# One selection matmul fills the inputs of two experts, where a transpose filled one

## Chip, cores and metric

The kernel runs on one core of a Trainium2 chip. The metric is the device time of one execution in microseconds (us).

## The reference

One layer of a decoder trunk on 320 tokens (256 of a prompt, 64 of samples), width 2048, all fp32. A token mixer comes first; the change does not touch it. Then a mixture of experts in two levels: each token goes to one of 4 groups, and there to 2 of 4 SwiGLU experts.

```python
g_val, g_idx = lax.top_k(g_prob, 1)
e_val, e_idx = lax.top_k(e_prob, TOP_K_EXPERT)
gates = g_val * e_val
combine = jnp.sum(jax.nn.one_hot(ids, N_EXPERTS, dtype=jnp.float32) * gates[..., None], axis=1)
hg = jnp.einsum('nd,edf->nef', xt, w_gate)      # 16 experts, D = 2048, F = 512
hu = jnp.einsum('nd,edf->nef', xt, w_up)
a = jax.nn.silu(hg) * hu * combine[:, :, None].astype(x.dtype)
out = jnp.einsum('nef,efd->nd', a, w_down)
x = layer_norm(ALPHA * x + out, ln2_g, ln2_b)
```

Every expert has 12 MB of weights (gate 4 MB, up 4 MB, down 4 MB), 192 MB in all, and each is read once.

## The kernel before

The mixer and its projections take roughly the first 395 us, the router the next 25, and the rest is the loop over the 16 experts, with which the change deals.

**Weights.** A ring of `SLOTS = 9` slots of 2 MB holds the experts' weights. The list `ORDER` gives the units in which they come: of expert e four units of gate and up (two transfers of 1 MB each), then the two down units of expert e-1 (one transfer of 2 MB each). SP issues the transfers in that order, in `load_half` (L380) and in `sp_experts` (L1060). From the tenth unit on it waits on `ring_used` for the matmuls that last read the slot. Before the tenth unit it waits for the gather of the first group's rows (L1049) and issues four loads of 1 MB for the layer norms (L1050 to L1053).

**Inputs of an expert.** The rows of one group of experts, up to 128 tokens, are gathered into `xg`. DVE's `pick(g)` writes `order` (L1486): for each of the group's four experts a matrix of zeros and ones that says which row stands at which of the expert's 64 places (`C = 64`); it is made 128 columns wide. It then makes `gated` from it. PE's `fill(e, j)` (L1189) makes four tiles of 128 features by 128 places for expert e, with a transpose that takes `order` in place of the identity; j runs over `FILLS = 4`, so that an expert needs 16 of them. ScalarE's `evict_fill(e, j)` (L1327) applies scale and bias of the layer norm and writes the first 64 columns of each to `xT[e % 2]`, one instruction per tile.

**PE's order.** All four fills of expert 0 stand ahead of the loop. In the loop over e, `gate_up(e, j)` (L1239, eight matmuls of 64 by 512, which read one unit) and `fill(e + 1, j)` take turns. Then come `turn_a(e - 1)` (L1249, transposes of the activations), `combine(e - 2)` (L1215), for the second expert of a group `weights_back(g)` (L1198), and `down(e - 1)` (L1263, 16 matmuls, which read the two down units). Behind the loop the same for the last expert, and `last_rows` (L1226).

**PSUM.** The fills of expert 0 use banks 0 to 3; all others use bank 7 (`MS`), so that `fill(e, j)` waits on `xT_ready` for the eviction of the fill before it.

**ScalarE's order.** For expert e: the evictions of fills 0 to 2 of expert e + 1, the Silu of expert e (L1361), the eviction of fill 3, the copy `aT` (L1334), for which `down` waits, and the copy `y_sb` (L1345).

Of the kernel before, what the change touches and what calls it, by code (L numbers as in the profile page):

```python
# [10 lines left out]
P = 128  # L11
# [26 lines left out]
def hybrid_trunk_kernel(nc, x_prompt, x_sample, state_conv, state_pool, w_in, conv_w, sgu_ln_g,  # L38
# [149 lines left out]
    G0 = YT_HI0  # L188
    xT = [at(f"xT{s}", G0 + s * 4 * KB, [P, PAIRS, 4, C]) for s in range(2)]
    y_sb = at("y_sb", G0 + 8 * KB, [P, HD])  # L190
    group_slot = at("group_slot", G0 + 12 * KB, [P, 3, P])
    order = at("order", G0 + 13 * KB + 512, [P, EG, P])
    gated = at("gated", G0 + 15 * KB + 512, [P, EG, 2, C])
# [977 lines left out]
    def pe_experts(pe):  # L1171
# [6 lines left out]

        def fill(e, j):

            g, k = where(e)
            pe.wait_ge(xn_ready, 2 * g + j // 2 + 1)
            pe.wait_ge(order_ready, g + 1)
            if e:
                pe.wait_ge(xT_ready, FILLS * e + j)
                pe.wait_ge(gatedT_ready, (e + 1) // EG)
            for c in range(4):
                col = HD * (j // 2) + 4 * (j % 2) + c
                last = pe.transpose(ps[:, fill_bank(e, j), P * c:P * (c + 1)],  # L1189
                                    xg[g % 2][:, col:HD * (j // 2 + 1):HK], order[:, k, :])  # L1190
            last.then_inc(xT_full, 1)

        def weights_back(g):

            pe.wait_ge(gated_ready, g + 1)
            pe.wait_ge(xT_ready, FILLS * (EG * g + 3))
            for k in range(EG):
                last = pe.transpose(ps[:, MS, P * k:P * (k + 1)],  # L1198
                                    gated[:, k, :, :].rearrange("p h s -> p (h s)"), ident[:, :])
            last.then_inc(gatedT_full, 1)  # L1200
# [28 lines left out]
        def gate_up(e, j):  # L1229
            i = AT[e, j]  # L1230
            pe.wait_ge(xT_ready, FILLS * e + j + 1)
            if e and j == 0:
                pe.wait_ge(a_ready, e)
            pe.wait_ge(unit_full[i % SLOTS], all_in(i))
            w = gu_w[i % SLOTS][:, :, :].rearrange("p g (c f) -> p g c f", c=4)
            for c in range(4):
                x = xT[e % 2][:, j, c, :]
# [34 lines left out]
        info(0, FACTS, info_made)  # L1272
        for j in range(FILLS):
            fill(0, j)
        for e in range(NE):
            g, k = where(e)
            for j in range(PAIRS):
                gate_up(e, j)
                if e + 1 < NE:
                    fill(e + 1, j)  # L1280
                if k == 0 and j == 1 and g < NG - 1:
# [39 lines left out]
    def act_experts(act):  # L1321
        def evict_fill(e, j):
            n = FILLS * e + j + 1
            act.wait_ge(xT_full, n)
            for c in range(4):
                hc = 4 * (j % 2) + c
                last = act.activation(xT[e % 2][:, j, c, :], ps[:, fill_bank(e, j), P * c:P * c + C],  # L1327
                                      ACT.Identity, bias=gbT[:, 1, j // 2, hc:hc + 1],
# [24 lines left out]
        for e in range(NE):  # L1353
            g, k = where(e)
            if e + 1 < NE:
                for j in range(FILLS - 1):
                    evict_fill(e + 1, j)
# [4 lines left out]
            if e + 1 < NE:  # L1362
                evict_fill(e + 1, FILLS - 1)
            if e:
# [103 lines left out]
    def dve_experts(dve, steps, link, rows):  # L1468
# [11 lines left out]
        def pick(g):  # L1480

            dve.wait_ge(told_ready, g + 1)
            if g:
                dve.wait_ge(xT_full, FILLS * EG * g)
                dve.wait_ge(gatedT_full, g)
            dve.scalar_tensor_tensor(out=order[:, :, :], in0=slots[:, :].unsqueeze(1).to_broadcast([P, EG, P]),  # L1486
                                     scalar=row_no[:, 0:1],
                                     in1=told[:, g, 1:1 + EG].unsqueeze(2).to_broadcast([P, EG, P]),
                                     op0=ALU.subtract, op1=ALU.is_equal).then_inc(order_ready, 1)
            dve.wait_ge(order_ready, g + 1)  # L1490
            for h in range(2):
                last = dve.tensor_tensor(gated[:, :, h, :], order[:, :, 0:C],
                                         told[:, g, 1 + EG:1 + 2 * EG].unsqueeze(2).to_broadcast([P, EG, C]),
                                         ALU.mult)
# [11 lines left out]
        def residual_rows(g):  # L1506

            x = xg[g % 2]
            if g == 0:
                dve.wait_ge(aln_in, 32)  # L1510
                steps.inc(dve.tensor_scalar(aln_g[:, :], aln_g[:, :], ALPHA, None, ALU.mult))
                link(dve.tensor_scalar(aln_b[:, :], aln_b[:, :], ALPHA, None, ALU.mult))
            dve.wait_ge(xT_full, FILLS * EG * (g + 1))
            link(dve.tensor_tensor(x[:, :], x[:, :], aln_g[:, :], ALU.mult))
# [264 lines left out]
```

## Time and profile before

| what | value |
|---|---|
| median of three runs | 905.77 us (904.85 to 905.96) |
| the profiled execution | 904.5 us, its span 902.5 us |
| PE busy | 830.9 us, 92% of the span |
| DVE, ScalarE, GpSimd busy | 283.7, 255.2, 22.7 us |
| read from HBM | 267.23 MB |

The span runs from the first to the last instruction of the profile; 2.0 us of the time lie outside it. PE's busy time counts a matmul from start to end, and a PE that waits for weights between two matmuls is idle. An fp32 matmul stands in the trace as two records, a transpose as one.

### The profile page before, as it was taken

The page shows a single profiled execution, that of the slowest core. Times are in us where ns is not written, and L with a number is a line of the kernel's source. Part 1 is how long each engine was busy: PE and PEld are TensorE (multiplying, and loading weights), DVE is VectorE, ACT ScalarE, POOL GpSimd, SP SyncE. Part 2 cuts the span into 40 slices and gives each one's busy share as a digit, 9 for nine tenths or more (in the row PEclk, how much of TensorE's full clock was granted, in tenths as well). Part 3 has the DMA queues.
Part 4 walks back from the last instruction along what each step waited for, and adds up shares of the span by engine and source line. Part 5 has one row for each costly group of instructions (what it writes and reads, how often), then busy time and mean ns, then how long its engine had stood idle before and what let it go on. Part 6 is the DMA issues. An engine that isn't in the chain of part 4 may idle for free.

```text
span 902.5 us, 11139 instructions
## 1 busy us (share of the span) xinstructions
PE 830.9 (92%) x4709; PEld 556.6 (62%) x4709; DVE 283.7 (31%) x389; ACT 255.2 (28%) x452; POOL 22.7 (3%) x37
## 2 busy tenths in 40 slices
PE   6999999999999999985999999999999888897884
PEld 6989999999999999974333333333333233333231
DVE  5273375335664343535002100412004030031203
ACT  5243332333223232332322222322223121222101
POOL 0000000000001000001000000000000000000000
PEclk9999999999999999996999999999999999999998
DMA  9643653654454884378999999999999999999960
GB/s 298 182 140 120 200 181 121 206 186 139 145 163 150 294 285 139 119 265 356 421 424 427 420 423 424 425 420 423 424 426 419 423 424 424 420 425 424 423 295 31
DMA packets 81595, 271.96 MB, mean 301 GB/s; under 512 B 5577, under 2 KB 58271, under 8 KB 59592
## 3 DMA queue, kind: packets, MB, share of 16 engines
q1 hardware_dynamic: 78618, 263.12, 75.0%
q0 software_dynamic: 1856, 5.28, 1.5%
q10 hardware_dynamic: 1078, 2.94, 1.0%
q8 instruction: 33, 0.54, 0.2%
q14 instruction: 10, 0.08, 0.0%
HBM read 267.23 MB, written 11.54 MB: 309 GB/s over the span
## 4 chain that ended last, share of the span: by engine, by line
PE 66%; DMA 20%; SPq 5%; DVE 4%; ACT 3%; issue 1%; POOLq 0%; POOL 0%; ACTq 0%; DVEq 0%
PE ps L1239 15%; DMA gu_w<-in_expert_w_up 14%; PE ps L458 12%; PE ps L460 11%; PE ps L459 11%; PE ps L1263 8%; SPq L380 4%; DMA down_w<-in_expert_w_down 4%; PE ps L1189 3%; DMA raw<-in_w_in 1%; ACT xT L1327 1%; DMA raw<-in_w_out 1%; PE ps L1126 1%; PE ps L485 1%; PE ps L486 1%
## 5 line engine op out<-in xcount | busy, mean ns | idle before, releaser
L1239 PE MATMUL ps<-gu_w,xT 128*64 128x512 f32 x1024 | 235.3, 601 | 26.8 <-DMA gu_w<-in_expert_w_up 26.2
L639 DVE TENSOR_TENSOR w_lo<-raw,w_hi 128x2048 fp32r<-128x2048 f32 x50 | 114.6, 2291 | 172.3 <-ACT w_hi L631 170.7
L1239 PEld LDWEIGHTS ps<-gu_w,xT 128*64 128x64 f32 x1024 | 74.9, 137 | 151.4 <-issue 146.6
L458 PE MATMUL ps<-xT_hi,w_hi 128*128 128x320 f32 x512 | 159.2, 311 | 0.0
L459 PE MATMUL ps<-xT_lo,w_hi 128*128 128x320 f32 x512 | 158.2, 309 | 0.0
L460 PE MATMUL ps<-xT_hi,w_lo 128*128 128x320 f32 x512 | 158.2, 309 | 0.0
L631 ACT ACTIVATE w_hi<-raw 128x2048 fp32r<-128x2048 f32 x49 | 93.8, 1914 | 209.4 <-DMA raw<-in_w_in 128.3
L1327 ACT ACTIVATE xT<-ps,gbT 128x64 f32<-128x64 f32 x256 | 82.4, 408 | 162.4 <-PE ps L1189 162.4
L1263 PE MATMUL ps<-down_w,aT 128*64 128x512 f32 x512 | 115.3, 602 | 4.6 <-ACT aT L1334 4.0
L1569 DVE TENSOR_TENSOR a_sb<-ps,a_sb 128x256 f32<-128x256 f32 x16 | 6.8, 425 | 298.5 <-ACT a_sb L1361 298.5
L458 PEld LDWEIGHTS ps<-xT_hi,w_hi 128*128 128x128 f32 x512 | 96.1, 188 | 0.5
L459 PEld LDWEIGHTS ps<-xT_lo,w_hi 128*128 128x128 f32 x512 | 96.1, 188 | 0.0
L460 PEld LDWEIGHTS ps<-xT_hi,w_lo 128*128 128x128 f32 x512 | 96.1, 188 | 0.0
L1263 PEld LDWEIGHTS ps<-down_w,aT 128*64 128x64 f32 x512 | 35.6, 138 | 80.6 <-issue 65.9
L458 PE MATMUL ps<-yT_hi,w_hi 128*128 128x320 f32 x256 | 79.8, 312 | 0.6 <-DVE yT_lo L799 0.6
L460 PE MATMUL ps<-yT_hi,w_lo 128*128 128x320 f32 x256 | 79.1, 309 | 0.0
L459 PE MATMUL ps<-yT_lo,w_hi 128*128 128x320 f32 x256 | 79.1, 309 | 0.0
L1189 PEld LDWEIGHTS ps<-order,xg 128*128 128x128 f32 x256 | 34.6, 197 | 52.4 <-issue 47.9
L1189 PE MATMUL ps<-order,xg 128*128 128x128 f32 x256 | 46.4, 308 | 3.6 <-DVE xg L1503 3.0
L458 PEld LDWEIGHTS ps<-yT_hi,w_hi 128*128 128x128 f32 x256 | 48.1, 188 | 0.9 <-DVE yT_lo L799 0.9
L459 PEld LDWEIGHTS ps<-yT_lo,w_hi 128*128 128x128 f32 x256 | 48.1, 188 | 0.0
L460 PEld LDWEIGHTS ps<-yT_hi,w_lo 128*128 128x128 f32 x256 | 48.1, 188 | 0.0
(241 smaller groups left out, 479.7 us busy)
## 6 DMA issues: line engine op xcount, KB each, us to landing
gu_w<-in_expert_w_gate SPq DMA_DIRECT2D x64, 1024.0 KB, 27.5
gu_w<-in_expert_w_up SPq DMA_DIRECT2D x64, 1024.0 KB, 30.9
down_w<-in_expert_w_down SPq DMA_DIRECT2D x32, 2048.0 KB, 31.2
raw<-in_w_in SPq DMA_DIRECT2D x34, 1024.0 KB, 5.3
raw<-in_w_out SPq DMA_DIRECT2D x16, 1024.0 KB, 5.4
tok<-in_x_prompt SPq DMA_DIRECT2D x2, 1024.0 KB, 6.2
z_rows<-tok ACTq DMA_DIRECT2D x2, 768.0 KB, 4.1
aln_g<-in_ln_g SPq DMA_DIRECT2D x1, 1024.0 KB, 4.2
```

The source lines that it names most:

```text
L380: sp.dma_start(gu_w[s][:, n, :].rearrange("p (c f) -> p c f", c=4), src[:, e, h, c:c + 4, :])\
L458: pe.matmul(out, wh[:, t, col], hi[:, kt, :], start=(n == 0 and t == 0), stop=False)
L459: pe.matmul(out, wh[:, t, col], lo[:, kt, :], start=False, stop=False)
L460: last = pe.matmul(out, wl[:, t, col], hi[:, kt, :], start=False, stop=(n == 1 and t == CK - 1))
L485: pe.matmul(out, wh[:, t, col], hi[:, kt, :], start=(n == 0 and t == 0), stop=False)
L486: pe.matmul(out, wh[:, t, col], lo[:, kt, :], start=False, stop=False)
L631: act.activation(w_hi[k][:, :], raw[k][:, :], ACT.Copy).then_inc(hi_ready, 1)
L639: dve.tensor_tensor(w_lo[k][:, :], raw[k][:, :], w_hi[k][:, :].bitcast(FP32), ALU.subtract)\
L1189: last = pe.transpose(ps[:, fill_bank(e, j), P * c:P * (c + 1)], xg[g % 2][:, col:HD * (j // 2 + 1):HK], order[:, k, :])
L1239: last = pe.matmul(ps[C * side:C * (side + 1), GU, :], x, w[:, :, c, FH * side:FH * (side + 1)], start=(j == 0 and c == 0), stop=(j == PAI ...
L1263: last = pe.matmul(ps[C * side:C * (side + 1), Y + q, :], aT[:, f % 2, f // 2, :], down_w[i % SLOTS][:, n, col:col + 512], start=(f == 0), ...
L1327: last = act.activation(xT[e % 2][:, j, c, :], ps[:, fill_bank(e, j), P * c:P * c + C], ACT.Identity, bias=gbT[:, 1, j // 2, hc:hc + 1], s ...
```

## The change

- `fill(pair, j)` takes the place of `fill(e, j)`. It multiplies the rows of `xg` with the selection of two neighbouring experts at once: 64 + 64 = 128 columns. It is an ordinary fp32 matmul and no transpose.
- `order` has 64 columns per expert (it had 128), so that two experts' columns lie side by side. It is written at 256 elements per partition in place of 512.
- `xT` is one tile with a place for both experts. ScalarE writes both from one tile of PSUM, 128 elements per instruction in place of 64, half as many instructions.
- Fills stand in the loop at odd experts only: behind `gate_up(e, j)` for odd e comes `fill((e + 1) // 2, j)`, for experts e + 1 and e + 2.
- Of the first pair only `fill(0, 0)` stands ahead of the loop; `fill(0, j + 1)` stands ahead of `gate_up(0, j)`.
- The counts in the waits follow. `weights_back(g)` waits for the same eviction as before, the fills that stand just ahead of it.

```diff
-    order = at("order", G0 + 13 * KB + 512, [P, EG, P])
+    order = at("order", G0 + 13 * KB + 512, [P, EG, C])
...
+        def fill(pair, j):
+
+            g, k = where(2 * pair)
             pe.wait_ge(xn_ready, 2 * g + j // 2 + 1)
             pe.wait_ge(order_ready, g + 1)
-            if e:
-                pe.wait_ge(xT_ready, FILLS * e + j)
-                pe.wait_ge(gatedT_ready, (e + 1) // EG)
+            if pair:
+                pe.wait_ge(xT_ready, FILLS * pair + j)
+                pe.wait_ge(gatedT_ready, pair // 2)
             for c in range(4):
                 col = HD * (j // 2) + 4 * (j % 2) + c
-                last = pe.transpose(ps[:, fill_bank(e, j), P * c:P * (c + 1)],
-                                    xg[g % 2][:, col:HD * (j // 2 + 1):HK], order[:, k, :])
+                last = pe.matmul(ps[:, fill_bank(pair, j), P * c:P * (c + 1)],
+                                 xg[g % 2][:, col:HD * (j // 2 + 1):HK],
+                                 order[:, k:k + 2, :].rearrange("p k s -> p (k s)"), start=True, stop=True)
             last.then_inc(xT_full, 1)
...
-        for j in range(FILLS):
-            fill(0, j)
+        fill(0, 0)
         for e in range(NE):
             g, k = where(e)
             for j in range(PAIRS):
+                if e == 0 and j + 1 < FILLS:
+                    fill(0, j + 1)
                 gate_up(e, j)
-                if e + 1 < NE:
-                    fill(e + 1, j)
+                if e % 2 and e + 1 < NE:
+                    fill((e + 1) // 2, j)
...
-                last = act.activation(xT[e % 2][:, j, c, :], ps[:, fill_bank(e, j), P * c:P * c + C],
+                last = act.activation(xT[:, :, j, c, :],
+                                      ps[:, fill_bank(pair, j), P * c:P * (c + 1)].rearrange("p (k s) -> p k s", k=2),
                                       ACT.Identity, bias=gbT[:, 1, j // 2, hc:hc + 1],
                                       scale=gbT[:, 0, j // 2, hc:hc + 1])
...
-            dve.wait_ge(xT_full, FILLS * EG * (g + 1))
+            dve.wait_ge(xT_full, FILLS * 2 * (g + 1))
```

The place at which the loop over the experts starts, on PE, before the change (`gu_w_52` to `gu_w_59` are slots of the ring; a row x4 is one fill, a row of `gu_w` x8 one `gate_up`):

```order
L1189 MATMUL ps<-order,xg_72 128x128 x16
L1239 MATMUL ps<-gu_w_52,xT_139 64x512 x8
L1189 MATMUL ps<-order,xg_72 128x128 x4
L1239 MATMUL ps<-gu_w_53,xT_139 64x512 x8
L1189 MATMUL ps<-order,xg_72 128x128 x4
L1175 MATMUL ps<-facts,group_slot 128x11 x3
L1239 MATMUL ps<-gu_w_54,xT_139 64x512 x8
L1189 MATMUL ps<-order,xg_72 128x128 x4
L1239 MATMUL ps<-gu_w_55,xT_139 64x512 x8
L1189 MATMUL ps<-order,xg_72 128x128 x4
L1239 MATMUL ps<-gu_w_56,xT_140 64x512 x8
```

The same place after it:

```order
L1189 MATMUL ps<-order,xg_72 128x128 x8
L1240 MATMUL ps<-gu_w_52,xT 64x512 x8
L1189 MATMUL ps<-order,xg_72 128x128 x4
L1240 MATMUL ps<-gu_w_53,xT 64x512 x8
L1175 MATMUL ps<-facts,group_slot 128x11 x3
L1189 MATMUL ps<-order,xg_72 128x128 x4
L1240 MATMUL ps<-gu_w_54,xT 64x512 x8
L1240 MATMUL ps<-gu_w_55,xT 64x512 x8
L1240 MATMUL ps<-gu_w_56,xT 64x512 x8
```

Two fills stand ahead of the first `gate_up` where there were four; the other two of the first pair stand behind the first and the second `gate_up`, and none stands behind the third and the fourth.

On ScalarE, from the fills of the first experts to the copy of `aT` of expert 0, before (`xT_139` and `xT_140` are the two buffers):

```order
L1327 ACTIVATE xT_139<-ps,gbT 128x64 x16
L1327 ACTIVATE xT_140<-ps,gbT 128x64 x12
L1361 ACT_TABLE_LOAD
L1361 ACTIVATE a_sb<-ps 128x256
L1327 ACTIVATE xT_140<-ps,gbT 128x64 x4
L1327 ACTIVATE xT_139<-ps,gbT 128x64 x12
L1361 ACTIVATE a_sb<-ps 128x256
L1327 ACTIVATE xT_139<-ps,gbT 128x64 x4
L1334 COPY aT<-ps 128x256
```

and after:

```order
L1329 ACTIVATE xT<-ps,gbT 128x2x64 x16
L1364 ACT_TABLE_LOAD
L1364 ACTIVATE a_sb<-ps 128x256
L1329 ACTIVATE xT<-ps,gbT 128x2x64 x12
L1364 ACTIVATE a_sb<-ps 128x256
L1329 ACTIVATE xT<-ps,gbT 128x2x64 x4
L1337 COPY aT<-ps 128x256
```

The evictions of expert 0's turn are gone, and those of expert 1's turn stand where they stood, four of them still between the Silu and the copy of `aT`, each twice as wide.

## Rows read from the trace of the kernel before

**Rows 1.** The page: GB/s in 40 equal slices of the span.

```profile
GB/s 298 182 140 120 200 181 121 206 186 139 145 163 150 294 285 139 119 265 356 421 424 427 420 423 424 425 420 423 424 426 419 423 424 424 420 425 424 423 295 31
```

**Rows 2.** Stretches: width, busy us of each engine, PEclk, DMA share, GB/s.

```profile
416.00:421.50 5.50, 1.56 (x6) 1.43 (x6) 3.61 (x14) 0.00 (x0) 0.00 (x0) 0.50 0.42 173
421.50:426.00 4.50, 3.96 (x18) 3.56 (x20) 1.21 (x2) 2.80 (x10) 0.00 (x0) 0.51 0.90 379
426.00:440.00 14.00, 14.00 (x72) 5.62 (x70) 0.46 (x4) 5.45 (x18) 1.03 (x1) 1.00 1.00 414
440.00:640.00 200.00, 195.56 (x922) 72.99 (x918) 32.12 (x43) 55.88 (x151) 3.06 (x3) 0.99 1.01 424
640.00:866.00 226.00, 196.81 (x903) 75.94 (x903) 36.09 (x47) 53.04 (x139) 5.01 (x5) 0.99 1.01 423
```

**Rows 3.** The chain that ended last: start us, us, what.

```profile
498.26 3.43 PE ps L1239 x16
...
524.33 3.43 PE ps L1239 x16
...
837.43 31.80 DMA down_w<-in_expert_w_down
...
869.27 3.68 PE ps L1263 x16
...
880.15 7.02 PE ps L1263 x32
```

**Rows 4.** Groups by shape on PE: count, busy us, mean ns, idle before.

```profile
L1239 PE MATMUL ps<-gu_w,xT 128*64 128x512 f32 x1024 | 235.3, 601 | 26.8 <-DMA gu_w<-in_expert_w_up 26.2 <-DVE a_sb L1569 0.5
...
L1189 PE MATMUL ps<-order,xg 128*128 128x128 f32 x256 | 46.4, 308 | 3.6 <-DVE xg L1503 3.0 <-issue 0.5
...
L574 PE MATMUL ps<-wsT,vtok 128*128 128x128 f32 x24 | 3.6, 273 | 0.0
```

**Rows 5.** The start of the experts in order of time: start, us, engine.

```profile
419.25 0.75 DVE L1486 SCALAR_TENSOR_TENSOR order<-slots,row_no,told 128x512 f32<-128x512 f32 x1
420.03 0.76 DVE L1492 TENSOR_TENSOR gated<-order,told 128x256 f32<-128x256 f32 x2
...
420.89 0.33 SPq L1050 DMA_DIRECT2D aln_g<-in_ln_g  x1
...
422.04 3.68 PE L1189 MATMUL ps<-order,xg 128*128 128x128 f32 x16 [3.04 <-DVE xg L1503]
...
429.32 0.71 PE L1189 MATMUL ps<-order,xg 128*128 128x128 f32 x4
...
429.96 3.65 PE L1239 MATMUL ps<-gu_w,xT 128*64 128x512 f32 x16
```

**Rows 6.** Groups by shape on ScalarE.

```profile
L1327 ACT ACTIVATE xT<-ps,gbT 128x64 f32<-128x64 f32 x256 | 82.4, 408 | 162.4 <-PE ps L1189 162.4
...
L709 ACT ACTIVATE pext<-ps 128x64 f32<-128x64 f32 x4 | 0.8, 266 | 0.0
...
L705 ACT ACTIVATE pnew<-ps 128x128 f32<-128x128 f32 x2 | 0.6, 296 | 0.0
```

**Rows 7.** In order of time, 460 to 470 us: SP's issues.

```profile
460.63 0.43 SPq L380 DMA_DIRECT2D gu_w<-in_expert_w_up  x1
...
468.81 0.33 SPq L380 DMA_DIRECT2D gu_w<-in_expert_w_gate  x1
```

**Rows 8.** DMA issues from 460 to 461 us: KB each, us to landing.

```profile
gu_w<-in_expert_w_up SPq DMA_DIRECT2D x1, 1024.0 KB, 14.8
```

**Rows 9.** PE in order of time, 701 to 711 us.

```profile
705.42 5.35 PE L1239 MATMUL ps<-gu_w,xT 128*64 128x512 f32 x16 [3.11 <-DMA gu_w<-in_expert_w_up]
```

**Rows 10.** Stretches around it and at expert 15, columns as in Rows 2.

```profile
844.00:864.00 20.00, 16.09 (x72) 5.67 (x70) 0.00 (x0) 1.25 (x2) 0.00 (x0) 1.00 1.02 428
...
705.00:709.00 4.00, 3.58 (x10) 1.44 (x12) 0.00 (x0) 0.00 (x0) 0.00 (x0) 0.59 1.03 438
```

**Rows 11.** PE in order of time, expert 15, where no fills stand.

```profile
859.58 3.65 PE L1239 MATMUL ps<-gu_w,xT 128*64 128x512 f32 x16 [1.31 <-DMA gu_w<-in_expert_w_up]
```

More of the change, by code:

```diff
@@ L188, in hybrid_trunk_kernel @@
     G0 = YT_HI0
-    xT = [at(f"xT{s}", G0 + s * 4 * KB, [P, PAIRS, 4, C]) for s in range(2)]
+    xT = at("xT", G0, [P, 2, PAIRS, 4, C])
     y_sb = at("y_sb", G0 + 8 * KB, [P, HD])
     group_slot = at("group_slot", G0 + 12 * KB, [P, 3, P])
-    order = at("order", G0 + 13 * KB + 512, [P, EG, P])
+    order = at("order", G0 + 13 * KB + 512, [P, EG, C])
     gated = at("gated", G0 + 15 * KB + 512, [P, EG, 2, C])
@@ L1177, in info @@
             last.then_inc(done, 1)
-        def fill(e, j):
-            g, k = where(e)
+        def fill(pair, j):
+            g, k = where(2 * pair)
             pe.wait_ge(xn_ready, 2 * g + j // 2 + 1)
             pe.wait_ge(order_ready, g + 1)
-            if e:
-                pe.wait_ge(xT_ready, FILLS * e + j)
-                pe.wait_ge(gatedT_ready, (e + 1) // EG)
+            if pair:
+                pe.wait_ge(xT_ready, FILLS * pair + j)
+                pe.wait_ge(gatedT_ready, pair // 2)
             for c in range(4):
                 col = HD * (j // 2) + 4 * (j % 2) + c
-                last = pe.transpose(ps[:, fill_bank(e, j), P * c:P * (c + 1)],
-                                    xg[g % 2][:, col:HD * (j // 2 + 1):HK], order[:, k, :])
+                last = pe.matmul(ps[:, fill_bank(pair, j), P * c:P * (c + 1)],
+                                 xg[g % 2][:, col:HD * (j // 2 + 1):HK],
+                                 order[:, k:k + 2, :].rearrange("p k s -> p (k s)"), start=True, stop=True)
             last.then_inc(xT_full, 1)
@@ L1195, in weights_back @@
             pe.wait_ge(gated_ready, g + 1)
-            pe.wait_ge(xT_ready, FILLS * (EG * g + 3))
+            pe.wait_ge(xT_ready, FILLS * (2 * g + 2))
             for k in range(EG):
@@ L1230, in gate_up @@
             i = AT[e, j]
-            pe.wait_ge(xT_ready, FILLS * e + j + 1)
+            pe.wait_ge(xT_ready, FILLS * (e // 2) + j + 1)
             if e and j == 0:
@@ L1236, in gate_up @@
             for c in range(4):
-                x = xT[e % 2][:, j, c, :]
+                x = xT[:, e % 2, j, c, :]
                 for side in range(2):
@@ L1321, in act_experts, with evict_fill @@
     def act_experts(act):
-        def evict_fill(e, j):
-            n = FILLS * e + j + 1
+        def evict_fill(pair, j):
+            n = FILLS * pair + j + 1
             act.wait_ge(xT_full, n)
@@ L1354, in act_experts @@
             g, k = where(e)
-            if e + 1 < NE:
+            if e % 2 and e + 1 < NE:
                 for j in range(FILLS - 1):
-                    evict_fill(e + 1, j)
+                    evict_fill((e + 1) // 2, j)
             act.wait_ge(ring_used, AT[e, PAIRS - 1] + 1)
@@ L1361, in act_experts @@
             act.activation(a_sb[:, :], ps[:, GU, 0:FH], ACT.Silu).then_inc(silu_ready, 1)
-            if e + 1 < NE:
-                evict_fill(e + 1, FILLS - 1)
+            if e % 2 and e + 1 < NE:
+                evict_fill((e + 1) // 2, FILLS - 1)
             if e:
@@ L1483, in pick @@
             if g:
-                dve.wait_ge(xT_full, FILLS * EG * g)
+                dve.wait_ge(xT_full, FILLS * 2 * g)
                 dve.wait_ge(gatedT_full, g)
-            dve.scalar_tensor_tensor(out=order[:, :, :], in0=slots[:, :].unsqueeze(1).to_broadcast([P, EG, P]),
+            dve.scalar_tensor_tensor(out=order[:, :, :], in0=slots[:, 0:C].unsqueeze(1).to_broadcast([P, EG, C]),
                                      scalar=row_no[:, 0:1],
-                                     in1=told[:, g, 1:1 + EG].unsqueeze(2).to_broadcast([P, EG, P]),
+                                     in1=told[:, g, 1:1 + EG].unsqueeze(2).to_broadcast([P, EG, C]),
                                      op0=ALU.subtract, op1=ALU.is_equal).then_inc(order_ready, 1)
@@ L1491, in pick @@
             for h in range(2):
-                last = dve.tensor_tensor(gated[:, :, h, :], order[:, :, 0:C],
+                last = dve.tensor_tensor(gated[:, :, h, :], order[:, :, :],
                                          told[:, g, 1 + EG:1 + 2 * EG].unsqueeze(2).to_broadcast([P, EG, C]),
```

## The prediction

> **What bounds the kernel now.** PE is busy for 92% of the span, which invites the thought that every microsecond taken from PE is won. So I read first what is moved from HBM, slice by slice [rows 1]. From slice 20 on, at some 429 us (a slice is 22.6 us), the traffic stands at 419 to 427 GB/s and stays there to slice 38. The stretches say the same more finely [rows 2]: a hole between 416 and 421.5 us (DMA share 0.42), in which SP waits for the gather and has issued nothing, then a share of 0.90, and from 426 to 866 us a share of 1.00 to 1.01 at 414 to 424 GB/s. The engines of the DMA are full for 440 us without a break. An expert's 12 MB (12.58 million bytes) at 423 GB/s take 29.7 us. PE, where it doesn't wait, needs 26.1 us for an expert: from the first `gate_up` of one at 498.26 to that of the next at 524.33 [rows 3]. So PE catches up with the weights and then waits for them, 26.2 us in all, in front of `gate_up` [rows 4].
>
> The chain of waits closes the case at its end [rows 3]: a down unit that was issued at 837.43 lands 31.8 us later, at 869.27 PE starts on it, and from there to the end of the span, 33 us, PE, ScalarE, DVE and GpSimd follow one another without a fill. The time is therefore made of three parts: the start up to 426 us, a stream of weights at a fixed rate, and a tail behind the landing of `down(14)`'s second unit. A change counts if it moves the start of the stream, lets it run dry, or touches the tail.
>
> **The records of the fills.** Before there are 64 fills of four transposes, 256 records [rows 4]. After there are 32 fills of four matmuls of two records each, again 256, over 128 columns again. One record costs 0.160 us at full clock now: a fill at 429.32 and the `gate_up` behind it at 429.96 are 0.64 us apart [rows 5]. An ordinary fp32 matmul of the same shape stands at L574: 3.6 us for 24 records, 0.150 each [rows 4]. From below I take this 0.150, and from above 0.308, the mean length of a fill's record if nothing overlapped [rows 4]. I choose 0.160, since the strided weights from `xg` are those of the fills. Then a fill costs 1.28 us in place of 0.64, there are half as many, and PE's sum doesn't change. What changes is the place: an odd expert pays 16 x 0.16 = 2.6 us more, an even one 2.6 us less.
>
> **ScalarE.** It issues 128 evictions in place of 256. One of 128 columns takes 296 ns where one of 64 takes 266 [rows 6], 0.03 us more. The total of 82.4 us [rows 6] about halves, and some 40 us of ScalarE's work vanish. They lie beside matmuls and end no wait of the chain in the tail. Only at odd experts do the four evictions between Silu and `aT` stay, with 4 x 0.03 = 0.1 us more, for which `down` waits. I count it with PE's delay below. Were the cover gone, it would be seven times 0.1 us.
>
> **The start.** `order` is written at 256 elements in place of 512. The 512 take 0.75 us, the two writes of 256 behind it 0.76 us together [rows 5], so some 0.35 us go, on the chain to the first fill at 422.04. Ahead of the first `gate_up` stand 16 records before (16 transposes) and 16 after (eight matmuls), 3.68 us at half clock [rows 5, 2]. The first `gate_up` ends, and frees the first slot, 0.35 us sooner. This gives nothing at the end: the hole of [rows 2] ends with the layer norms' loads, which wait for the gather and not for PE, and they keep the stream full until the first freed slot.
>
> **Does the stream run dry later?** PE falls behind in experts 0 and 1. With 0.64 us for each added half of a fill: the second slot comes free 0.3 us later than now (0.64 - 0.35), the third 0.9 us (1.28 - 0.35), the fourth 0.3 us, since no fill stands behind the third `gate_up`. At expert 1 come four times 0.64 us and the 0.1 us of ScalarE. So its `turn_a` and the release by the first down unit, at 468.81 now [rows 7], come 0.3 + 2.6 + 0.1 = 3.0 us later, at 471.8. The load issued before it, at 460.63, lands 14.8 us later, at 475.4 [rows 7, 8]. That leaves 3.6 us of cover; a new load needs about 1.1 us before bytes move (the layer norms' loads are issued from 420.9 on [rows 5], and from 421.5 to 426 a tenth of the time is still missing [rows 2]). The spare is 2.5 us: the stream doesn't stop. This is the tightest place. Behind it PE gains 2 x 29.7 - 2 x 26.1 = 7.2 us on the stream with each two experts [rows 2, 3].
>
> In the stretch where PE waits for weights, an odd expert needs 26.1 + 2.6 + 0.1 = 28.8 us, still under 29.7; if PE also waits for the evictions ahead of `down` it falls behind by a microsecond, which the even expert gives back. SP's issues go on meanwhile: 31.8 us from issue to landing [rows 3] are six units queued.
>
> **The end.** Expert 15 has no fills before or after. At expert 14 the four fills of 0.64 us go; they lie in the wait for weights. The landing at 869.27 is set by the rate of the stream, and nothing behind it is edited. `residual_rows` and `pick` may start sooner, in idle time of DVE.
>
> **Sum.** Start 0, stream 0, tail 0: 904.5 us by the profiled execution's own time, which lies 1.3 us under the median of the runs shown, 905.77. I forecast 905.6 us, a hair under that median since one of the three runs and the profiled execution lie lower.
>
> **Rivals.** A change of less than 0.2%, 1.8 us, can't be told from none here.
>
> *The stream runs dry (slower).* The place is expert 1's `down`, the mechanism a matmul record dearer than 0.16 us. 48 records of fills run there at full clock, and the spare of 2.5 us is used up at 0.16 + 2.5 / 48 = 0.212 us a record. At 0.308 the delay is 48 x 0.148 = 7.1 us more, of which 4.6 us are lost: 905.8 + 4.6 = 910.4. For it: strided weights twice per matmul. Against it: 0.150 at L574. 4 in 100.
>
> *The clock falls in the tail (slower).* After a wait of 3.11 us at 705.42 one `gate_up` took 5.35 us in place of 3.65, and the granted clock of that stretch was 0.59, so partly 1.2 GHz [rows 9, 10]. The change takes the fills out of even experts, so that expert 14 waits 1.3 us in front of each `gate_up` where it waited 0.7. It decides if the clock is at 1.2 GHz after 869.27, where PE's work is on the path. Price: 1.7 us by the row, 907.5; were it low for all of the first 19 us, nearly 19 us. Against it: expert 15 already waits 1.31 us each time [rows 11] and the clock reads 1.00 from 844 to 864 us [rows 10]; in mid-stream a slow `gate_up` is made good. 6 in 100. The Trainium skill (TensorE: Matmul & The Clock Gate, "HAM oscillation — how this bites in real kernels") describes this: waits for transfers between bursts of matmuls throw the clock back to half, and every burst begins slow. [...]
>
> *It is faster.* If matmuls in the first fills bring the clock up sooner than transposes do, 16 records gain up to 0.230 - 0.150 = 0.08 us each, 1.3 us, and with DVE's 0.35 us the first slot comes 1.6 us sooner. The stretch from 426 to 440 us moves 414 GB/s, 2% under the 424 behind it [rows 2]: an earlier load can win at most 0.02 x 14 = 0.3 us, 905.5, within what can't be told. To be faster by 1.8 us the stream of 450 us would have to run 0.4% quicker with less traffic of ScalarE beside it; its stretches now differ by 424 to 423 while ScalarE works equally in both [rows 2], so nothing speaks for it. 5 in 100. The Trainium skill (same page, "Part 4: PE-mode transpose") states that work in transpose mode doesn't count as activity for the clock. By that rule the clock would rise sooner after the change; here 16 transposes ran at about half clock until 426 us, which fits the rule and doesn't prove it, and the time would be the 905.5 of this rival.
>
> **How the numbers follow.** No change: 85 in 100, own range 904.2 to 907.2, the spread of the runs shown with half a microsecond on either side. Dry stream 4, clock in the tail 6, faster 5. The range that leaves out no more than 2 in 10 reaches toward both: 903.9 to 907.6, which takes in the clock's 907.5. Faster by over 0.2%: 0.05; within: 0.85; slower: 0.10.
>
> **What would show it.** In the profile after: 256 records at the fill's line with about 0.16 us each; ScalarE's `xT` group near 42 us with 128 instructions; the traffic from 426 to 866 us at 423 GB/s and a share of 1.00; PE's wait for `gu_w` still 20 to 35 us, now mostly at even experts; the landing before `down(14)`'s second unit at 869 us, and 33 us from there to the end. Wrong would be a stretch between 460 and 480 us with a DMA share under 0.95, a granted clock under 1.00 after 869 us, or that landing more than 1.8 us away from 869.

## The result, and the profile after

The changed kernel takes 911.89 us (median of four runs, 910.4 to 912.16) against 905.31 us for the kernel before in the same session (904.67 to 905.96): 6.6 us more by the medians. The ratio of the runs compared is 1.0062, with an interval of 1.0046 to 1.0078. The forecast was 905.6 us, in a range of 903.9 to 907.6. The profiled execution's span is 910.3 us (902.5 before).

The page of the changed kernel shows the surprise at once. First the traffic in the 40 slices, then groups of instructions (busy us, mean ns, idle before), which answer to [rows 4] and [rows 6]:

```profile
GB/s 292 184 139 120 208 168 138 187 184 147 164 150 167 295 243 138 167 266 336 398 397 368 419 424 425 426 419 424 425 424 420 424 424 423 421 423 424 424 292 30
...
L1240 PE MATMUL ps<-gu_w,xT 128*64 128x512 f32 x1024 | 232.0, 602 | 2.7 <-DMA gu_w<-in_expert_w_up 1.6
...
L1189 PEld LDWEIGHTS ps<-order,xg 128*128 128x128 f32 x256 | 63.3, 333 | 38.4 <-issue 21.9
...
L1189 PE MATMUL ps<-order,xg 128*128 128x128 f32 x256 | 69.5, 420 | 14.7 <-DVE xg L1506 14.7
L1329 ACT ACTIVATE xT<-ps,gbT 128x128 f32<-128x128 f32 x128 | 48.2, 459 | 132.9 <-PE ps L1189 132.9
```

There are 256 records of fills as forecast, but they take 69.5 us in place of 46.4, and their weight loads last 333 ns where they lasted 197 before:

```profile
L1189 PEld LDWEIGHTS ps<-order,xg 128*128 128x128 f32 x256 | 34.6, 197 | 52.4 <-issue 47.9
```

PE's wait for the gate and up weights is down from 26.2 us to 1.6, where 20 to 35 were forecast. ScalarE's evictions went from 82.4 to 48.2 us. In the row of GB/s, slices 20 to 22 stand at 398, 397 and 368, where 421, 424 and 427 were moved before [rows 1].

The same in order of time, at expert 2's fills (start, us):

```profile
515.17 2.17 PE L1189 MATMUL ps<-order,xg 128*128 128x128 f32 x8
517.27 3.65 PE L1240 MATMUL ps<-gu_w,xT 128*64 128x512 f32 x16
```

A fill of eight records takes 2.10 us, from 515.17 to 517.27: 0.262 us a record, not 0.160. This is the measure of the prediction, from the start of a fill to the start of what follows. Busy time divided by records is another one and gives 0.271 here (69.5 / 256); where it is used below, the text says so. The stretches of the changed kernel (width, busy us of PE, weight loads, DVE, ScalarE and GpSimd, PEclk, DMA share, GB/s) answer to [rows 2]:

```profile
416.00:421.50 5.50, 1.55 (x6) 1.43 (x6) 3.54 (x16) 0.00 (x0) 0.18 (x1) 0.50 0.54 223
421.50:426.00 4.50, 2.89 (x12) 2.89 (x13) 1.66 (x3) 0.57 (x2) 0.00 (x0) 0.50 0.58 218
426.00:440.00 14.00, 14.00 (x59) 7.80 (x58) 0.46 (x4) 3.96 (x11) 0.51 (x1) 0.88 0.99 394
440.00:460.00 20.00, 18.85 (x83) 8.86 (x82) 0.42 (x1) 4.68 (x10) 0.52 (x1) 1.00 1.00 413
...
470.00:480.00 10.00, 7.98 (x33) 4.03 (x34) 0.89 (x2) 2.63 (x7) 0.00 (x0) 0.83 0.72 277
480.00:500.00 20.00, 20.00 (x96) 6.59 (x92) 2.26 (x4) 1.66 (x3) 0.00 (x0) 1.00 0.98 401
500.00:560.00 60.00, 59.72 (x270) 25.13 (x268) 8.93 (x12) 9.24 (x22) 0.00 (x0) 1.00 1.01 423
```

Two of these stretches in the kernel before, which [rows 2] has only as part of a longer one:

```profile
470.00:480.00 10.00, 10.00 (x49) 3.37 (x46) 0.00 (x0) 2.31 (x5) 0.00 (x0) 1.00 1.01 422
480.00:500.00 20.00, 19.93 (x96) 7.47 (x97) 10.15 (x10) 5.44 (x15) 0.00 (x0) 1.00 1.01 424
```

From 500 us on the stream of weights is as full as before. What it lost, it lost ahead of that: from 470 to 500 us (422 - 277) x 10 + (424 - 401) x 20 = 1,910, at 423 GB/s 4.5 us. The four stretches from 416 to 460 us lack another 2.4 us against before: 50 x 5.5 gained, and 161 x 4.5, 20 x 14 and 15 x 20 lost (428 GB/s before from 440 to 460). That makes 6.9 of the 7.7 us by which this profiled execution is longer than the one before (912.16 against 904.5); the rest isn't placed. The 2.4 us can't be put down to the loss: the profiles of e1, e3 and e8 below lack 2.0, 2.5 and 2.1 us in the same stretches, and their times are those of the kernel before. From 470 to 500 us these three lack 0.1 us at most. Cut finer, the place shows itself:

```profile
476.00:477.00 1.00, 1.00 (x4) 0.24 (x2) 0.00 (x0) 0.00 (x0) 0.00 (x0) 0.50 0.85 360
477.00:478.00 1.00, 1.00 (x6) 0.28 (x4) 0.00 (x0) 0.00 (x0) 0.00 (x0) 0.93 0.39 164
478.00:479.00 1.00, 1.00 (x8) 0.28 (x5) 0.00 (x0) 0.00 (x0) 0.00 (x0) 1.00 0.16 66
479.00:480.00 1.00, 1.00 (x8) 0.42 (x6) 0.00 (x0) 0.00 (x0) 0.00 (x0) 1.00 0.00 0
480.00:481.00 1.00, 1.00 (x8) 0.28 (x4) 0.00 (x0) 0.00 (x0) 0.00 (x0) 1.00 0.38 74
```

Why it is empty there, SP's issues in order of time tell, with [rows 7] as the counterpart:

```profile
469.84 0.43 SPq L380 DMA_DIRECT2D gu_w<-in_expert_w_up  x1
...
479.63 0.33 SPq L380 DMA_DIRECT2D gu_w<-in_expert_w_gate  x1
```

and the landing of the first of the two, in the view of the DMA issues from 469 to 471 us (KB, us to landing):

```profile
gu_w<-in_expert_w_up SPq DMA_DIRECT2D x1, 1024.0 KB, 9.5
```

The load issued at 469.84 lands at 479.3. The next is issued at 479.63, when expert 1's `down` gives its first slot back. Before, these two moments were 475.4 and 468.81, in the other order. The gate load of the same unit, issued at 469.47, lands 7.4 us later, at 476.9. From then on only one load is left, and the share is 0.39 from 477 to 478 us and 0.16 behind it: the stream is thin some 2 us ahead of the last landing. The end of the chain of waits then carries the loss to the end, 7.74 us later than in [rows 3] at the landing:

```profile
844.54 32.42 DMA down_w<-in_expert_w_down
877.01 3.68 PE ps L1264 x16
...
887.89 7.02 PE ps L1264 x32
```

### The profile page after: what moved, and what is told of

Its sections match the earlier page's. It is cut to its first block, busy times and chain, and to the rows that moved or that the text cites. A ratio compares the mean times of both kernels' runs of the same rounds, so it can differ in the third digit from the quotient of the medians.

```text
span 910.3 us, 10947 instructions
## 1 busy us (share of the span) xinstructions
PE 854.0 (94%) x4709; PEld 583.9 (64%) x4709; DVE 282.8 (31%) x389; ACT 221.9 (24%) x324; POOL 22.7 (2%) x37
## 4 chain that ended last, share of the span: by engine, by line
PE 79%; DMA 11%; DVE 4%; ACT 3%; issue 2%; POOL 0%; POOLq 0%; SPq 0%; DVEq 0%; ACTq 0%
PE ps L1240 20%; PE ps L458 12%; PE ps L459 11%; PE ps L460 11%; PE ps L1264 10%; PE ps L1189 7%; DMA down_w<-in_expert_w_down 4%; DMA xg<-z_rows,row 3%; DMA out<-xg,sample_row 2%; PE ps L1216 2%; DMA raw<-in_w_in 1%; DVE xg L1558 1%; DMA raw<-in_w_out 1%; PE ps L1126 1%; PE ps L485 1%
## 5 line engine op out<-in xcount | busy, mean ns | idle before, releaser
L1240 PE MATMUL ps<-gu_w,xT 128*64 128x512 f32 x1024 | 232.0, 602 | 2.7 <-DMA gu_w<-in_expert_w_up 1.6
L1240 PEld LDWEIGHTS ps<-gu_w,xT 128*64 128x64 f32 x1024 | 72.3, 139 | 140.4 <-issue 137.6
L1189 PEld LDWEIGHTS ps<-order,xg 128*128 128x128 f32 x256 | 63.3, 333 | 38.4 <-issue 21.9
L1189 PE MATMUL ps<-order,xg 128*128 128x128 f32 x256 | 69.5, 420 | 14.7 <-DVE xg L1506 14.7
L1329 ACT ACTIVATE xT<-ps,gbT 128x128 f32<-128x128 f32 x128 | 48.2, 459 | 132.9 <-PE ps L1189 132.9
```

The costliest lines, as they stand in the source:

```text
L1189: last = pe.matmul(ps[:, fill_bank(pair, j), P * c:P * (c + 1)], xg[g % 2][:, col:HD * (j // 2 + 1):HK], order[:, k:k + 2, :].rearrange("p ...
L1240: last = pe.matmul(ps[C * side:C * (side + 1), GU, :], x, w[:, :, c, FH * side:FH * (side + 1)], start=(j == 0 and c == 0), stop=(j == PAI ...
L1329: last = act.activation(xT[:, :, j, c, :], ps[:, fill_bank(pair, j), P * c:P * (c + 1)].rearrange("p (k s) -> p k s", k=2), ACT.Identity, ...
```

## The experiments

Each ran beside the kernel before on the same chip; ratios are against that. Those named e edit `fill` alone; those named v keep the whole computation and look for a gain, or for the reason why there is none.

**e1_contiguous.** Neighbouring columns of `xg` as the stationary operand.

```diff
-                                 xg[g % 2][:, col:HD * (j // 2 + 1):HK],
+                                 xg[g % 2][:, P * (4 * j + c):P * (4 * j + c + 1)],
```

> The changed kernel, but each fill's stationary operand is 128 neighbouring columns of xg in place of 128 columns at a distance of 8 (so it leaves out the right order of the features). Theory S (the step between the columns of the stationary operand makes the fill's record dear, and the lost time is the stream of weights running dry): a record of the fill costs 0.11 to 0.15 us in place of 0.262, LDWEIGHTS about 0.19 us in place of 0.335, the DMA share from 470 to 480 us is 0.95 or more, time 905 to 906.5 us. Rival M (an ordinary fp32 matmul of 128 columns costs 0.26 us here whatever its operands' steps): the record stays at 0.26 us and the time at 911 to 912 us.

Measured: 905.88 us, ratio 1.0 (0.9987 to 1.0012). The by-shape groups of its matmuls and weight loads, and the stretch where the changed kernel's stream ran dry:

```profile
L1189 PE MATMUL ps<-order,xg 128*128 128x128 f32 x256 | 39.4, 301 | 9.0 <-DVE xg L1506 9.0
```

```profile
L1189 PEld LDWEIGHTS ps<-order,xg 128*128 128x128 f32 x256 | 33.3, 204 | 32.7 <-issue 22.7 <-DVE xg L1506 10.0
```

```profile
470.00:480.00 10.00, 10.00 (x50) 3.41 (x48) 0.00 (x0) 1.01 (x1) 0.00 (x0) 1.00 1.01 419
```

A fill takes 1.09 us here (the one at 509.01 is followed by a `gate_up` at 510.10), 0.136 us a record in place of 0.262. By busy time it is 0.154 (39.4 / 256) in place of 0.271. The same instructions, at the same places, in the same number; only the step of an operand is gone, and with it the whole loss. Rival M falls.

**e3_contiguous_first_two and e4_strided_first_two.** The dear fills at one end of the loop or at the other.

```diff
-                last = pe.matmul(ps[:, fill_bank(pair, j), P * c:P * (c + 1)],
-                                 xg[g % 2][:, col:HD * (j // 2 + 1):HK],
+                block = P * (4 * j + c)
+                rows = xg[g % 2][:, block:block + P] if pair < 2 else xg[g % 2][:, col:HD * (j // 2 + 1):HK]
+                last = pe.matmul(ps[:, fill_bank(pair, j), P * c:P * (c + 1)], rows,
```

In e4 the condition is `pair >= 2`.

> The changed kernel, with neighbouring columns as the stationary operand in the fills of the first two pairs (experts 0 to 3) only; all later fills as in the changed kernel (leaves out the right order of the features there). Theory D (the time is lost where the stream of weights runs dry at 470 to 500 us, and the dear fills later cost nothing): 905.5 to 907 us, DMA share 0.95 or more from 470 to 480 us. Rival P (PE as a whole has become the bound, 0.1 us more per record wherever it stands): 910 to 911 us, since only 64 of 256 records are cheaper.

> The opposite: columns at a distance of 8 in the first two pairs' fills as in the changed kernel, neighbouring columns in the fills of pairs 2 to 7 (leaves out the right order of the features there). Theory D: 910.5 to 912 us, the stream runs dry at 470 to 480 us as in the changed kernel. Rival P: 906 to 908 us, since 192 of 256 records are cheaper.

Measured: e3, with 192 dear records of 256, 905.73 us, ratio 0.9993 (0.9981 to 1.0005). e4, with only 64 dear ones, 909.98 us, half a microsecond under the expected range, ratio 1.0059 (1.0039 to 1.0079), the changed kernel's own ratio within the interval. Their stretches, e3 first:

```profile
470.00:480.00 10.00, 10.00 (x48) 3.30 (x46) 0.00 (x0) 1.01 (x1) 0.00 (x0) 1.00 1.00 415
```

```profile
470.00:480.00 10.00, 8.12 (x40) 3.06 (x42) 0.89 (x2) 3.01 (x8) 0.00 (x0) 1.00 0.81 306
```

The loss belongs to the first two pairs, and to the dry stretch. A quarter of the records is enough for it; the other three quarters cost PE 24 us in e3 (63.0 us busy in its fills against 39.4 in e1) that nobody waits for. Theory D holds, rival P falls.

The dry stretch is shallower in e4, though: (422 - 306) x 10 - (429 - 424) x 20 = 1,060, 2.5 us at 423 GB/s, where the changed kernel lost 4.5. A lower clock fits most of the difference. These are `weights_back` and `down` in expert 1's turn (start, us, and in brackets the wait before), in the changed kernel and in e4:

```profile
473.78 1.09 PE L1199 MATMUL ps<-ident,gated 128*128 128x128 f32 x4 [2.02 <-ACT xT L1329]
474.80 8.23 PE L1264 MATMUL ps<-down_w,aT 128*64 128x512 f32 x32
```

```profile
471.88 0.63 PE L1200 MATMUL ps<-ident,gated 128*128 128x128 f32 x4 [2.02 <-ACT xT L1330]
472.44 7.09 PE L1265 MATMUL ps<-down_w,aT 128*64 128x512 f32 x32
```

Behind the same wait of 2.02 us for ScalarE the granted clock of the changed kernel reads 0.50 until 477 us, that of e4 1.00, and PE needs 1.6 us more in the changed kernel. The clock fell at this place before the change as well (0.83 from 460 to 470 us), and in e6; it stayed at 1.00 in e1, e3, e7, e8 and v5. Nothing here shows what decides it. It is not the cause of the loss, since e4 loses without it and the kernel before loses nothing with it, but it makes PE later where the cover is thinnest.

**e7_strided_pair_one.** The step of 8 in pair 1 alone (`pair != 1` as the condition).

> The changed kernel with a step of 8 in the fills of pair 1 alone (those that stand in expert 1's turn) and neighbouring columns everywhere else (leaves out the right order of the features there). Theory D: PE is some 2.5 us earlier at expert 1's down units than with both pairs strided, since 16 full-speed records and 16 at half clock of pair 0 are cheaper; the dip of the DMA share from 470 to 480 us is smaller than in the changed kernel (0.72) and the time 906.5 to 909 us. If pair 0 were what matters: 905.5 us; if its share were nothing: 910 us or more.

Measured: 906.59 us, ratio 1.0012 (0.9999 to 1.0024), the share from 470 to 480 us 0.91 at 351 GB/s. With half of the dear records in front of the tight place the dip is between none and the full one: (422 - 351) x 10 - (430 - 424) x 20 = 590, 1.4 us at 423 GB/s. The time itself can't be told from that of the kernel before.

**e6_strides.** One step for each of a fill's four matmuls, on lines of their own. `h0` is the first column of the half of `xg`, `sel` the selection of the two experts.

```diff
+                    last = pe.matmul(ps[:, fill_bank(pair, j), P * c:P * (c + 1)], xg[g % 2][:, h0:h0 + 1 * P:1], sel, start=True, stop=True)
...
+                    last = pe.matmul(ps[:, fill_bank(pair, j), P * c:P * (c + 1)], xg[g % 2][:, h0:h0 + 2 * P:2], sel, start=True, stop=True)
```

and so on with steps of 4 and 8.

> The changed kernel, with the four matmuls of each fill on lines of their own and with steps of 1, 2, 4 and 8 elements between the columns of the stationary operand (leaves out the right order of the features). Theory S in its plain form (the cost grows with the step): LDWEIGHTS 0.19 us at step 1, something between at 2 and 4, 0.335 at 8. Rival T (any step over 1 is dear alike): 0.19 at step 1 and 0.335 at 2, 4 and 8. Rival M: 0.335 at all four.

Measured: 906.92 us in its only run. The weight loads by shape, in the order of steps 8, 4, 2 and 1:

```profile
L1198 PEld LDWEIGHTS ps<-order,xg 128*128 128x128 f32 x64 | 18.4, 336 | 0.0
L1196 PEld LDWEIGHTS ps<-order,xg 128*128 128x128 f32 x64 | 17.5, 321 | 0.0
L1194 PEld LDWEIGHTS ps<-order,xg 128*128 128x128 f32 x64 | 11.0, 214 | 0.0
L1192 PEld LDWEIGHTS ps<-order,xg 128*128 128x128 f32 x64 | 10.4, 203 | 36.8 <-issue 21.9 <-DVE xg L1513 14.8
```

None of the three theories had it. A step of 2 fp32 elements costs next to nothing (214 against 203 ns), a step of 4 nearly all (321), and 8 adds little (336). The theory that the cost grows evenly with the step and rival T are both out. In order of time the two records at step 2 take 0.23 us until the next start, the two at step 4 take 0.47:

```profile
508.96 0.49 PE L1192 MATMUL ps<-order,xg 128*128 128x128 f32 x2
509.29 0.40 PE L1194 MATMUL ps<-order,xg 128*128 128x128 f32 x2
509.52 0.63 PE L1196 MATMUL ps<-order,xg 128*128 128x128 f32 x2
509.99 0.64 PE L1198 MATMUL ps<-order,xg 128*128 128x128 f32 x2
```

**e8_eight_transposes.** The placement of the change at the price that the prediction took.

```diff
-                last = pe.matmul(ps[:, fill_bank(pair, j), P * c:P * (c + 1)],
-                                 xg[g % 2][:, col:HD * (j // 2 + 1):HK],
-                                 order[:, k:k + 2, :].rearrange("p k s -> p (k s)"), start=True, stop=True)
+                for k2 in range(2):
+                    last = pe.transpose(ps[:, fill_bank(pair, j), P * c:P * (c + 1)],
+                                        xg[g % 2][:, col:HD * (j // 2 + 1):HK], ident[:, :])
```

> The changed kernel with its place and number of fills, but each of a fill's four matmuls of two records replaced by two transposes against the identity, at the same step of 8 in xg (leaves the selection of the tokens out). So 256 records remain where the change puts them, at the price the prediction took. If that price is the step of the prediction that failed: 0.16 us a record, LDWEIGHTS 0.19 us, a DMA share of 0.95 or more from 470 to 480 us, 905 to 906.5 us. If the placement at odd experts were itself at fault: 908 us or more at 0.16 us a record.

Measured: 906.67 us, ratio 1.0001 (0.9988 to 1.0015), a share of 1.00 from 470 to 480 us. Its groups by shape, matmuls and weight loads:

```profile
L1190 PE MATMUL ps<-ident,xg 128*128 128x128 f32 x256 | 39.1, 300 | 8.1 <-DVE xg L1506 8.1
```

```profile
L1190 PEld LDWEIGHTS ps<-ident,xg 128*128 128x128 f32 x256 | 32.9, 196 | 31.8 <-issue 22.7 <-DVE xg L1506 9.0
```

At the very step of 8, a transpose's weight load takes 196 ns where the matmul's takes 333. A fill takes 1.08 us (506.27 to 507.35), 0.135 us a record, or 0.153 by busy time (39.1 / 256). The time is a hair above the expected 905 to 906.5 us, beside a kernel before that took 906.15 us in that session. Everything else that the change does costs nothing that the times can show, as forecast.

**e5_matmul_alone.** The kernel before with ordinary matmuls in place of its transposes, without the pairing.

```diff
-                last = pe.transpose(ps[:, fill_bank(e, j), P * c:P * (c + 1)],
-                                    xg[g % 2][:, col:HD * (j // 2 + 1):HK], order[:, k, :])
+                last = pe.matmul(ps[:, fill_bank(e, j), P * c:P * (c + 1)],
+                                 xg[g % 2][:, col:HD * (j // 2 + 1):HK], order[:, k, :], start=True, stop=True)
```

> The kernel before with one part of the change: an ordinary fp32 matmul in place of each fill's transpose, one expert per fill as before, so 512 records. Theory S with 0.262 us a record: a fill costs 2.1 us in place of 0.64, an expert 26.1 + 4 x 1.46 = 31.9 us of PE against 29.7 us of the stream; PE becomes the bound and the time 940 to 955 us. Rival (the record is dear only at odd experts' places in the changed kernel, through what stands beside it): a record under 0.2 us and a time of 905 to 915 us.

Measured: 961.73 us, ratio 1.0615 (1.0595 to 1.0635), beyond the expected 940 to 955 us. Its group has the changed kernel's price per record, 138.1 / 512 = 0.270 us by busy time against 0.271:

```profile
L1189 PE MATMUL ps<-order,xg 128*128 128x128 f32 x512 | 138.1, 415 | 3.0 <-DVE xg L1503 3.0
```

So the price hangs on the kind of instruction together with the step, and neither the pairing nor the place of the fills is needed for it. Here the pairing isn't there to halve it, PE is the bound at 32.4 to 33.1 us an expert (its `down` starts at 834.45, 866.86 and 899.95 in the chain of waits), and every microsecond counts.

**v1_two_loads_early, v2_one_load_early.** On the kernel before: is the hole from 416 to 421.5 us worth anything?

```diff
-                sp.wait_ge(lgT_made, 1)
+                sp.wait_ge(facts_ready, 1)
+                sp.dma_start(lng[:, :], ln2_g[0:1, :].to_broadcast([P, D])).then_inc(ln2_in, 16)
+                sp.dma_start(lnb[:, :], ln2_b[0:1, :].to_broadcast([P, D])).then_inc(ln2_in, 16)
                 sp.wait_ge(gathered, 16)
```

The two loads go from behind the wait for the gather; v2 moves `lng` alone.

> The kernel before, with the loads lng and lnb issued as soon as facts_ready is set (about 416.7 us) and not behind the wait for the gather, so that they fill the hole in the stream from 417 to 421.5 us. If the stream is the bound from there to the end: 2.5 to 3.5 us faster, 902 to 903 us. Rival: the gather lands later beside them, PE starts later by 2 us or more and the stream runs dry near 470 us: 904 to 906 us.

> The same with one load only (lng). If the stream is the bound: 1.5 to 2.5 us faster, 903 to 904 us, with less delay of the gather than with two.

Measured: v1 905.83 us, ratio 0.9997 (0.9985 to 1.0009); v2 905.37 us, ratio 0.9991 (0.9979 to 1.0004). No gain, and not for the rival's reason either. The gather landed in time (`aln_g`, which waits for it, is issued at 420.95). Stretches of v1:

```profile
416.00:421.50 5.50, 1.56 (x6) 1.43 (x6) 3.61 (x14) 0.00 (x0) 0.00 (x0) 0.50 0.94 387
...
426.00:440.00 14.00, 14.00 (x72) 5.72 (x70) 0.46 (x4) 5.62 (x19) 1.03 (x1) 1.00 0.92 343
```

The hole is filled (0.42 before [rows 2]), and opens again behind: from 426 to 440 us 343 GB/s where 414 were moved. The early loads are done early, and the next can't be issued before the first slot comes free at 429. What the stream gains ahead of that slot it loses behind it: the slot's release by PE's first `gate_up` sets its start, and the loads of the layer norms only fill the time up to it.

**v4_two_fills_ahead, v3_both.** On the kernel before: two fills ahead of the first `gate_up`, later ones two units ahead of their use; v3 has v1's loads too.

```diff
-        for j in range(FILLS):
+        for j in range(AHEAD):
             fill(0, j)
...
-                if e + 1 < NE:
-                    fill(e + 1, j)
+                if FILLS * e + j + AHEAD < FILLS * NE:
+                    fill(*divmod(FILLS * e + j + AHEAD, FILLS))
```

> The kernel before (transposes, one expert per fill), with two fills in place of four ahead of the first gate_up and each later fill two units ahead of its use. The first slot comes free up to 1.8 us sooner. Theory N (with the layer norms' loads behind the gather the queue is still full then): no gain, 905 to 906 us.

> The same together with the two loads issued early (v1). Each alone gives nothing: one moves the hole behind itself, the other frees slots for a queue that is full. Together they should close both: 1 to 2 us faster, 903.5 to 905 us, the DMA share from 426 to 440 us at 0.97 or more where v1 had 0.92.

Measured: v4 905.75 us, ratio 0.9994 (0.9984 to 1.0005), as expected, but its first slot came free at 429.05, hardly sooner than the 429.43 of the kernel before. So v4 doesn't test what an earlier release is worth. v3 905.59 us, ratio 1.0 (0.9987 to 1.0013), against my expectation of 1 to 2 us, and its share from 426 to 440 us is 0.83 at 308 GB/s, not 0.97. Its PE in order of time:

```profile
420.34 1.97 PE L1190 MATMUL ps<-order,xg 128*128 128x128 f32 x8 [3.04 <-DVE xg L1504]
422.84 5.40 PE L1240 MATMUL ps<-gu_w,xT 128*64 128x512 f32 x16 [0.53 <-ACT xT L1328]
```

Its two fills are half as long as the four [rows 5], but then the first `gate_up` takes 5.40 us and not 3.7: it runs in the stretch in which the granted clock is 0.50, 1.2 GHz. From the start of the first fill to the release of the first slot pass 428.29 - 420.34 = 7.95 us, and 429.43 - 422.04 = 7.4 before. The slow clock's work is only exchanged for other work at the slow clock.

**v5_step_two.** A version of the change with the whole computation, whose fills have a step of 2.

```diff
+    gate_2 = w_gate[0].rearrange("e (q p c) f -> p e q c f", q=HK, c=2)
...
+        sp.dma_start(gu_w[s][:, n, :].rearrange("p (q x) -> p q x", q=2),
+                     src[:, e, 2 * u:2 * u + 2, :, :].rearrange("p q c f -> p q (c f)"))\
...
-                                 xg[g % 2][:, col:HD * (j // 2 + 1):HK],
+                                 xg[g % 2][:, col:2 * P * (2 * j + c // 2 + 1):2],
```

> The change with the whole computation kept, and the features dealt to the partitions so that the stationary operand of a fill has a step of 2 in place of 8: gate and up weights are loaded as two runs of 4 KB per partition in place of one of 8 KB, and the layer norm's scale and bias likewise. Theory S: LDWEIGHTS about 0.21 us, a record about 0.12 us, no dip of the DMA share from 470 to 480 us, 905 to 906.5 us, level with the kernel before and 5 us under the changed kernel. Rival: the shorter runs slow the stream (under 420 GB/s from 500 to 866 us), one per cent being 4.5 us: 908 us or more.

Measured: 915.56 us, ratio 1.0109 (1.009 to 1.0128), slower than the changed kernel. Group of its fills, and its long stretches:

```profile
L1193 PE MATMUL ps<-order,xg 128*128 128x128 f32 x256 | 40.9, 307 | 7.4 <-DVE xg L1510 7.4
```

```profile
470.00:480.00 10.00, 10.00 (x50) 3.32 (x48) 0.00 (x0) 1.01 (x1) 0.00 (x0) 1.00 1.00 404
...
500.00:640.00 140.00, 135.19 (x640) 52.66 (x636) 20.37 (x30) 29.36 (x67) 3.06 (x3) 0.98 1.02 414
640.00:866.00 226.00, 194.22 (x882) 73.59 (x880) 35.39 (x46) 36.03 (x77) 5.00 (x5) 0.98 1.02 415
```

The fills are cheap again, 1.14 us each (506.38 to 507.52), 0.142 us a record where 0.12 was expected, and the share doesn't dip. But the rival came true: the stream runs at 414 to 415 in place of 423 GB/s, 2% over some 440 us, 9 us. The gate and up weights, two thirds of the bytes, come in runs half as long. The layout made the fills cheap for PE and the weights dear for the DMA, and the DMA is the bound.

No version beat the kernel before by more than the measurement tells.

## Why the prediction was wrong, step by step

- *The engines of the DMA are full for 440 us, and the time is start, stream and tail:* right, and it is the frame in which the loss was found. The share from 500 to 866 us is 1.01 at 422 to 424 GB/s after the change as well, and the tail from the landing to the end has the same 33 us (877.01 to 910.3).
- *One record costs 0.160 us:* this step failed. I weighed the strided weights, and took the fills' own transposes as the nearest row for them, since they have the same step. The row had the right step and the wrong kind of instruction. L574 had the right kind (0.150) and no step. Neither row had both, and both together cost 0.262 us. The two effects don't add up from the two rows: e1 (matmul, no step) and e8 (transpose, step 8) came to 0.136 and 0.135 us a record, and only the matmul with the step is dear. The upper bound of 0.308 held it. With 0.262 the rival's own sum gives 48 x 0.102 - 2.5 = 2.4 us lost and 908.2 us, already outside the range; the 911.89 measured need the next step as well.
- *Does the stream run dry:* the place was right, expert 1's `down` against a load that lands at 475.4. The cover was sized too generously. The prediction took the time from the release to the landing, less 1.1 us for a new load, as spare. In e4 the last load lands at 477.7 (467.94 + 9.8) and the release comes at 476.13, 1.6 us ahead of it. By that count 0.5 us were spare, but the stream is all but dry before the release:

```profile
475.00:476.00 1.00, 1.00 (x8) 0.36 (x6) 0.00 (x0) 0.00 (x0) 0.00 (x0) 1.00 0.26 107
476.00:477.00 1.00, 1.00 (x8) 0.36 (x6) 0.00 (x0) 0.00 (x0) 0.00 (x0) 1.00 0.10 41
```

In e6 the release comes 2.7 us ahead of the landing (473.92 and 476.6), and the share from 470 to 480 us is still 0.91; in e1 it comes 6.6 us ahead (469.80 and 476.4), and the share is 1.01. So the cover that is needed lies between 2.7 and 6.6 us and not at 1.1, and of the forecast 3.6 us at most 0.9 were spare. The rival's point of 0.212 us a record becomes 0.18 or less (0.16 + 0.9 / 48). Its chance of 4 in 100 was far too small for a cost that no row showed, and the range stopped short of that rival's bound.
- *PE is 3.0 us later there:* it was 10.8 us (479.63 against 468.81). 48 records x 0.102 us are 4.9. The first slot came free 2.5 us later (431.96 against 429.43) and not 0.35 sooner: the first fill began 1.1 us later (423.11 against 422.04), since the gather landed about 1.4 us later (`aln_g` issued at 422.28 and not 420.89), the first 16 records took 4.19 us and not 3.68, the first `gate_up` 4.6 and not 3.7. In sum 3.0 + 4.9 + 2.5 + 0.35 = 10.8. The late gather isn't the change's doing: `aln_g` is issued anywhere between 420.2 and 422.4 us in e1 to e8, none of which edits anything ahead of it. e8 had the same late start (its first slot free at 431.72), and its stream shows no dip, so the late start alone is covered; it counts once the price has used the cover up. The release that the prediction started from, 468.81, already had the slow clock in it, as the changed kernel's has.
- *The clock falls in the tail:* no; the granted clock from 866 to 880 us is 1.00, and it stays there up to 896 us, where PE's work ends. That a slow clock in mid-stream is made good doesn't hold everywhere: at expert 1's `down`, where the cover is thinnest, it made PE 1.6 us later.
- *The matmuls bring the clock up sooner at the start:* no. From 426 to 440 us the granted clock is 0.88 with matmuls in the fills, 0.92 with e8's transposes, and was 1.00 before; e4 and e5, with matmuls at the same step, read 1.00 as well. By the rule of the Trainium skill (TensorE: Matmul & The Clock Gate, "Part 4: PE-mode transpose") that transposes don't count as activity, it should have risen sooner with matmuls; these rows don't show it, though e8 and the change also began a microsecond or two later than the kernel before.
- *ScalarE's evictions near 42 us:* 48.2, with 459 ns for 128 columns against 408 for 64: 0.05 us more each, not 0.03. Off the path as forecast.
- *Nothing at the layer norms' loads:* right, and v1 and v2 confirm that an earlier load alone doesn't move the end. v3 released its first slot at 428.29, 1.1 us sooner, and gained nothing either.

What stays open is why a weight load is dear from a step of 4 elements on, and so much dearer in an ordinary fp32 matmul. The step isn't free for a transpose either: with neighbouring columns, at L607 of the kernel before, its load takes 140 ns (mean of 32), at a step of 8 196 or 197. The traces show the durations and no cause.

## What to carry to other kernels

Before a transpose becomes a matmul, look for a row that has both the new kind of instruction and the old step of the stationary operand; where none has, the upper bound belongs into the range, and the point at which it decides into the chances. In a kernel bound by a stream of loads, ask of every engine's extra work where the cover is thinnest: 64 dear records in front of that place cost some 5 us (e4), 192 behind it cost nothing (e3). Don't count the cover up to the landing of the last load: the stream thins out before it. A remedy has to be priced at the bound, too: the layout that made the fills cheap halved the DMA's runs and lost 9 us.

## What was unexpected of the hardware

- The weight load of an ordinary fp32 matmul of 128 columns took 203 ns at a step of 1 element, 214 at 2, 321 at 4 and 336 at 8 (e6). That of a transpose took 196 ns at a step of 8 (e8) and 140 at a step of 1 (L607 of the kernel before).
- Weights loaded in runs of 4 KB in place of 8 KB moved 414 to 415 GB/s in place of 423 to 424, at a DMA share that read 1.02 (v5).
- With one load left, the DMA share fell to 0.26 and 0.10 in the two microseconds ahead of its landing at 477.7 us (e4).
- Behind one and the same wait of 2.02 us the granted clock stood at 0.50 in the changed kernel and in e6, and at 1.00 in e1, e3, e4, e7 and e8.
- A hole in the stream that is filled opens again a few microseconds later if the ring's first release doesn't move (v1).
